# A transformer layer on one core: seven block products instead of eight for 7 of the 22 k-pairs of the down projection

## What is computed

```python
def conv_ffn(h, w_up, conv_w, conv_b, w_down):
    u = h @ w_up                                   # 2048 -> 11264
    ...
    a, b = jnp.split(u, 2, axis=-1)
    return (jax.nn.silu(a) * b) @ w_down           # 5632 -> 2048

def reference(x, ...):
    h = rms_norm(x, attn_norm[l]); p = h @ w_in[l]
    ...
    x = x + mix @ w_out[l]
    h = rms_norm(x, ffn_norm[l])
    x = x + conv_ffn(h, w_ffn_up[l], ffn_conv_w[l], ffn_conv_b[l], w_ffn_down[l])
```

## Time and profile before

| | |
|---|---|
| median of 3 runs | 1104.97 us (1104.68 to 1104.99) |
| span of the profiled execution, first to last instruction | 1103.2 us |
| PE busy | 1097.5 us, 99% of the span |
| DVE busy / ACT busy | 784.8 us (71%) / 586.6 us (53%) |
| down projection, first to last matmul start | 860.01 to 1099.14 us |
| from memory | 201.5 MB, 185 GB/s over the span |

### The profile page before, as it was taken

The page is one execution under the profiler, slowest core; times in us unless marked ns, Lnnn a source line. Parts: engine busy times, 40 slices in busy tenths (PEclk is TensorE's granted clock), DMA queues, the critical chain, the costliest instruction groups (busy, mean ns, idle before and its releaser), DMA issues.

```text
span 1103.2 us, 18805 instructions
## 1 busy us (share of the span) xinstructions
PE 1097.5 (99%) x6633; PEld 946.9 (86%) x6633; DVE 784.8 (71%) x1174; ACT 586.6 (53%) x863; POOL 26.8 (2%) x40
## 2 busy tenths in 40 slices
PE   9999999999999999999999999999999999999998
PEld 8888888888888888888888888888888888888887
DVE  6878988979656587878787878787878644454443
ACT  6677675766555555555455555555555433333332
POOL 4500000000000000000000000000000000000000
PEclk9999999999999999999999999999999999999999
DMA  7544556555555665556555565655555556656562
GB/s 260 188 153 145 162 173 190 166 183 172 181 183 167 191 196 189 188 190 190 190 190 190 184 191 183 191 185 190 188 190 190 191 191 198 208 195 214 193 210 76
DMA packets 172514, 204.26 MB, mean 185 GB/s; under 512 B 6949, under 2 KB 140470, under 8 KB 172214
## 3 DMA queue, kind: packets, MB, share of 16 engines
q1 hardware_dynamic: 171302, 201.55, 57.1%
q10 hardware_dynamic: 1168, 2.11, 0.6%
HBM read 201.54 MB, written 2.10 MB: 185 GB/s over the span
## 4 chain that ended last, share of the span: by engine, by line
PE 99%; DVE 1%; ACT 0%; issue 0%; DVEq 0%; ACTq 0%
PE bank L1344 37%; PE bank L1352 19%; PE bank L1398 10%; PE bank L1397 10%; PE bank L1396 10%; PE bank L1566 3%; PE bank L1567 3%; PE bank L1568 3%; PE bank L1310 1%; PE bank L1315 1%; PE bank L1605 0%; PE bank L1485 0%; PE bank L1373 0%; PE bank L1375 0%; PE bank L1376 0%; DVE hs L855 0%
## 5 line engine op out<-in xcount | busy, mean ns | idle before, releaser
L824 DVE TENSOR_TENSOR w_lo<-raw,w_hi 128x1024 fp32r<-128x1024 f32 x379 | 461.7, 1222 | 255.1 <-ACT w_hi L467 254.5
L467 ACT CAST w_hi<-raw 128x1024 fp32r<-128x1024 f32 x379 | 397.1, 1051 | 404.5 <-PE bank L1398 174.5
L1344 PE MATMUL bank<-hs,w_hi 128*128 128x512 f32 x1792 | 430.9, 391 | 0.0
L1344 PEld LDWEIGHTS bank<-hs,w_hi 128*128 128x128 f32 x1792 | 328.6, 188 | 64.1 <-issue 0.9
L1352 PEld LDWEIGHTS bank<-hs,w_lo 128*128 128x128 f32 x1792 | 230.1, 191 | 8.9 <-issue 0.2
L1352 PE MATMUL bank<-hs,w_lo 128*128 128x256 f32 x1792 | 233.9, 283 | 0.0
L1396 PE MATMUL bank<-w_hi,gated 128*128 128x512 f32 x352 | 136.9, 389 | 0.0
L1397 PE MATMUL bank<-w_lo,gated 128*128 128x512 f32 x352 | 136.9, 389 | 0.0
L1398 PE MATMUL bank<-w_hi,gated 128*128 128x512 f32 x352 | 136.9, 389 | 0.0
L1396 PEld LDWEIGHTS bank<-w_hi,gated 128*128 128x128 f32 x352 | 66.1, 188 | 13.8
L1397 PEld LDWEIGHTS bank<-w_lo,gated 128*128 128x128 f32 x352 | 66.1, 188 | 13.8
(11 more groups left out here) (188 smaller groups left out, 720.2 us busy)
## 6 DMA issues: line engine op xcount, KB each, us to landing
raw<-in_w_ffn_up_dram SPq DMA_DIRECT2D x176, 512.0 KB, 3.4
raw<-in_w_ffn_down_dram SPq DMA_DIRECT2D x88, 512.0 KB, 3.6
raw<-in_w_in_dram SPq DMA_DIRECT2D x52, 512.0 KB, 3.6
raw<-in_w_in_dram SPq DMA_DIRECT2D x64, 256.0 KB, 2.9
raw<-in_w_out_dram SPq DMA_DIRECT2D x32, 512.0 KB, 4.5
xt<-in_x_dram SPq DMA_DIRECT2D x2, 1024.0 KB, 6.6
out_dram<-xt ACTq DMA_DIRECT2D x3, 512.0 KB, 6.3
out_dram<-xt ACTq DMA_DIRECT2D x2, 256.0 KB, 2.5
```

The costliest lines, as they stand in the source:

```text
L467: act.copy(w_hi[:, i, :], raw[:, i, :]).then_inc(units_hi, 1)
L824: dve.tensor_tensor(w_lo[:, i, :], raw[:, i, :], w_hi[:, i, :].bitcast(F32), ALU.subtract)\
L1344: m = pe.matmul(banks[b][:, :], w_hi[:, i, c], hs[:, 4 * i + k, :], start=(first and k == 0), stop=(final and k == 3))
```

## The change

The output is now made as two pairs of column groups (`pair`, 1024 columns each). In a pair, four banks take two column blocks x two token halves, and k goes by in 22 k-pairs (`kp`, 2 k-tiles each; the code's `QUADRUPLES`). A unit is now 1 k-tile x 1024 columns, still 512 KB, and a k-pair is two units, a `four` or a `seven`:

- `four` (15 of 22): the two units are cast and split as before, and PE does 2 x 2 x 2 block products of three matmuls: 24 matmuls.
- `seven` (kp 6, 8, 10, 12, 14, 16, 18, in each of the two pairs): of the four weight blocks three are cast and split as they are (one operation of 128x1536 on ACT, one on DVE). DVE makes four sums of weight blocks (`t13` of 128x1024, then `t24` in two steps of 128x512), ACT casts them (`t_hi`), DVE makes their `lo` in place. PE does seven block products: 21 matmuls. Three of them are gathered over the pair in banks of their own (`bank_q5`, `bank_p6`, `bank_p7`, with `bank_p1` as the fourth) and merged into `xt` once a pair by DVE (`merge`, eight adds of 128x512).

The sums of activations that the sevens need (`s_hi`, `s_lo`) are made once, where `hs` stood, in four rounds (`sums_of_activations`, `hi_of_sums`, `lo_of_sums`): three in place of the k-pairs 1 to 3, which are split already, and the last after k-pair 4. The loops of the down projection are written out instead of being run by registers.

```diff
-            with sp.Fori(0, OUT_GROUPS // 2) as m:
...
+            for pair in range(COLUMN_PAIRS):
+                for kp in range(QUADRUPLES):
+                    for r in range(2):
+                        unit = first_unit_of(pair, kp) + r
+                        load_unit(unit // RING, unit % RING, w_down_v, 2 * kp + r, 1, pair * 2 * GT, 2 * GT)
...
+            def hi_of_sums(c):
+                act.wait_ge(s_made, c + 1)
+                n = min(2, SEVENS - 2 * c)
+                act.copy(s_hi[:, 2 * c:2 * c + n, :, :], sums[:, 0:n, :, :]).then_inc(s_rounded, 1)
+            def hi_of_plain(pair, kp):
...
+                act.wait_ge(loaded[i], loads_until(unit // RING) * 16)
+                act.wait_ge(loaded[i + 1], loads_until(unit // RING) * 16)
+                act.wait_ge(units_used, unit + 2)
+                act.copy(w_hi[:, i:i + 2, :].rearrange("p k n -> p (k n)")[:, GT:4 * GT],
+                         raw[:, i:i + 2, :].rearrange("p k n -> p (k n)")[:, GT:4 * GT]).then_inc(units_hi, 2)
+            def hi_of_summed(pair, kp):
...
+                act.wait_ge(t13_made, s + 1)
+                act.copy(t_hi[:, 0:2, :], t13[:, :, :]).then_inc(t13_hi, 1)
+                act.wait_ge(t4_made, s + 1)
+                act.copy(t_hi[:, 2:4, :], t24[:, :, :]).then_inc(t24_hi, 1)
...
+            for pair in range(COLUMN_PAIRS):
+                for kp in range(QUADRUPLES):
+                    if pair == 0 and kp < 4:
+                        if kp:
+                            hi_of_sums(kp - 1)
+                        continue
+                    hi_of(pair, kp)
+                    if pair == 0 and kp == 4:
+                        hi_of_sums(3)
+                    if kp == QUADRUPLES - 2:
+                        copy_partial(pair)
...
+            def lo_of_seven(pair, kp):
...
+                dve.wait_ge(units_hi, unit + 2)
+                dve.tensor_tensor(w_lo[:, i:i + 2, :].rearrange("p k n -> p (k n)")[:, plain],
+                                  raw[:, i:i + 2, :].rearrange("p k n -> p (k n)")[:, plain],
+                                  w_hi[:, i:i + 2, :].rearrange("p k n -> p (k n)")[:, plain].bitcast(F32),
+                                  ALU.subtract).then_inc(plain_split, 1)
...
+                dve.wait_ge(t_used, s)
+                dve.tensor_tensor(t13[:, :, :], quadruple[:, 1:3, :],
+                                  quadruple[:, 0:1, :].broadcast_to([P, 2, GT]), ALU.add).then_inc(t13_made, 1)
+                dve.wait_ge(t13_made, s + 1)
+                dve.sem_inc(units_split, 1)
+                dve.tensor_tensor(t24[:, 0, :], t13[:, 0, :], quadruple[:, 2, :], ALU.add).then_inc(t2_made, 1)
+                dve.wait_ge(t2_made, s + 1)
+                dve.tensor_tensor(t24[:, 1, :], t24[:, 0, :], quadruple[:, 3, :], ALU.add).then_inc(t4_made, 1)
+                dve.wait_ge(t13_hi, s + 1)
+                dve.tensor_tensor(t13_lo[:, :, :], t13[:, :, :], t_hi[:, 0:2, :].bitcast(F32), ALU.subtract)\
+                    .then_inc(t13_split, 1)
+                dve.wait_ge(t4_made, s + 1)
+                dve.sem_inc(units_split, 1)
+                dve.wait_ge(t24_hi, s + 1)
+                dve.tensor_tensor(t24_lo[:, :, :], t24[:, :, :], t_hi[:, 2:4, :].bitcast(F32), ALU.subtract)\
+                    .then_inc(t24_split, 1)
...
+            for pair in range(COLUMN_PAIRS):
+                for kp in range(QUADRUPLES):
+                    if pair == 0 and kp < 4:
+                        if kp:
+                            sums_of_activations(kp - 1)
+                            lo_of_sums(kp - 1)
+                        continue
+                    lo_of(pair, kp)
+                    if pair == 0 and kp == 4:
+                        sums_of_activations(3)
+                        lo_of_sums(3)
+                    if kp == QUADRUPLES - 2:
+                        merge(pair)
+                    if pair == 1 and kp == 0:
+                        add_last(0)
+            add_last(1)
...
+            def seven(pair, kp):
...
+                pe.wait_ge(plain_split, s + 1)
+                three(bank_p1(pair), *of_gated(2 * kp, 0), w_hi[:, i, c1], w_lo[:, i, c1], first, final)\
+                    .then_inc(units_used, 1)
+                three(bank_c(pair, 0, 1), *of_gated(2 * kp + 1, 0), w_hi[:, i + 1, c1], w_lo[:, i + 1, c1], False, False)
+                pe.wait_ge(s_split, n // 2 + 1)
+                three(bank_c(pair, 0, 0), *minus_sum_4, w_hi[:, i + 1, c0], w_lo[:, i + 1, c0], False, False)\
+                    .then_inc(units_used, 1)
+                pe.wait_ge(t13_split, s + 1)
+                three(bank_q5(pair), *sum_1, t_hi[:, 0, :], t13_lo[:, 0, :], first, final)
+                three(bank_p7(pair), *sum_3, t_hi[:, 1, :], t13_lo[:, 1, :], first, final)
+                pe.wait_ge(t24_split, s + 1)
+                three(bank_p6(pair), *sum_2, t_hi[:, 2, :], t24_lo[:, 0, :], first, final)
+                three(bank_c(pair, 1, 1), *of_gated(2 * kp + 1, 1), t_hi[:, 3, :], t24_lo[:, 1, :], False, False)\
+                    .then_inc(t_used, 1)
```

More of the change, by code:

```diff
@@ L798, in _ @@
             b_work(UP_GROUPS - 1, Q_DOWN + 1)
[L800 to L812, removed]
@@ L1710, in _, with three @@
                         unit_channels(g * 2 + ab + Q_UP, i, pair_of(G_UP + ab))
[L1713 to L1717, removed]
-                    if v == DOWN_UNITS - 1:
-                        pe.wait_ge(gated_lo, UP_GROUPS)
-                    unit_tokens(m * (2 * DOWN_UNITS // RING) + Q_DOWN + v // RING, v % RING,
-                                G_DOWN + n, gated, 2 * u, KT_FF, signal_first_tile=(u == DOWN_UNITS - 1))
+            def three(dst, x_hi, x_lo, hi, lo, start, stop):
+                pe.matmul(dst[:, :], x_hi, hi, start=start, stop=False)
+                pe.matmul(dst[:, :], x_hi, lo, start=False, stop=False)
+                return pe.matmul(dst[:, :], x_lo, hi, start=False, stop=stop)
@@ new lines, in of_gated, with four @@
+            def of_gated(tile, t):
+                return (gated[:, tile, t * P:(t + 1) * P], gated[:, tile, SEQ + t * P:SEQ + (t + 1) * P])
+            def four(pair, kp):
+                for r in range(2):
+                    unit = first_unit_of(pair, kp) + r
+                    i = unit % RING
+                    pe.wait_ge(units_split, unit + 1 + RING)
+                    for b in range(2):
+                        c = slice(b * GT, (b + 1) * GT)
+                        for t in range(TT):
+                            last = three(bank_c(pair, t, b), *of_gated(2 * kp + r, t), w_hi[:, i, c], w_lo[:, i, c],
+                                         kp == 0 and r == 0, kp == QUADRUPLES - 1 and r == 1)
+                            if kp == QUADRUPLES - 1 and r == 1 and (b, t) != LAST_BANKS[-1]:
+                                last.then_inc(bank_done, 1)
+                    last.then_inc(units_used, 1)
@@ new lines, in _ @@
+            for pair in range(COLUMN_PAIRS):
+                for kp in range(QUADRUPLES):
+                    if pair == 0 and kp == SEVEN_PRODUCTS[0]:
+                        pe.wait_ge(groups_evacuated, G_DOWN + BANK_PAIRS)
+                    if pair == 0 and kp == QUADRUPLES - 1:
+                        pe.wait_ge(gated_lo, UP_GROUPS)
+                    if pair == 1 and kp == 0:
+                        pe.wait_ge(merged, 1)
+                    if pair == 1 and kp == SEVEN_PRODUCTS[0]:
+                        pe.wait_ge(out_added, 4)
+                    if is_seven(kp):
+                        seven(pair, kp)
+                    else:
+                        four(pair, kp)
```

172 lines of the change are left out of this document (145 added, 27 removed).

## The result

| | before | after |
|---|---|---|
| median of the runs | 1104.9 us (5 runs, 1104.7 to 1105.0) | 1109.2 us (5 runs, 1108.8 to 1110.0) |
| span of the profiled execution | 1103.2 us | 1106.9 us |
| first and last matmul start of the down projection | 860.01, 1099.14 | 859.96, 1103.33 |

The ratio is 1.0041, with a 95% interval of 1.0030 to 1.0052: slower by 4.3 us, though PE has 42 matmuls less to do. The forecast was 1110.2 us, in a range of 1104.4 to 1117.

A forecast was written before the change was run, and what follows sets the result against it. The prediction took PE, busy 99% of the span, to bound the kernel. From 1104.97 us, -9.5 (matmuls), +8.1 (stop), +1.9 (clock), +0.2 (tail) and +4.5 (sevens) gave 1110.2 us, range 1104.4 to 1117.

The forecast's parts named there:

- What bounds the kernel, and the price of a matmul: PE, busy 99% of the span, bounds; 42 matmuls less in the down projection at 0.2267 us each: -9.5 us.
- The stop: PE stands still once ahead of unit 8, as three rounds of sums take 15.3 us against DVE's 8.4 lead: +8.1 us.
- the fourth round: Last round of sums, one k-pair, about 3 us, behind the split of units 8 and 9: 0 to 0.4 us.
- The clock: PE resumes at half clock after standing still at unit 8, for 3.8 us: +1.9 us, bounds 0 and 3.8.
- The sevens: Late second load makes the `raw` slot loop 10.65 us against PE's 10.20; ten waits of 0.45: +4.5 us, bounds 0 and 11.
- L: Landing time of a seven's second load, taken as 4.6 us; up to 4.2 PE would not wait.
- A page against the rows: Skill's 3.2 us for a 512 KB load gives a 9.2 us loop without PE waits; rows of paired loads contradict it.
- the rival of 1105.7: Pairs of loads land in time, up to 4.2 us, so the sevens run at PE's pace: 1105.7 us, chance 0.27.
- Hidden parts: `merge`, adding the first pair's four banks and ACT's 1 MB store stay covered among fours; written-out loops cost 0.
- The tail: Four stores of 256 KB at the end, issued 0.68 us apart, the last may queue: +0.2 us, bounds 0 and 0.8.
- The sum: Median before plus all terms: 1104.97 - 9.5 + 8.1 + 1.9 + 0.2 + 4.5 = 1110.2 us.

The follow-up runs named there:

- the layout run: Changed kernel with all 22 k-pairs as fours and no sums, merge or products of sums: 1103.9 us, ratio 0.9994 to the kernel before.
- both edits together: Changed kernel with rounds of sums among k-pairs 4 to 7 (13 sevens), and sums ahead of the plain `w_lo` in each seven: 1095.4 us, ratio 0.9919.
- the run with PE kept at work: Changed kernel plus 32 matmuls, result overwritten, that fill PE's stop ahead of unit 8: 1106.2 us, ratio 1.0013 to the kernel before.
- halves: Changed kernel with each down projection unit loaded by two transfers of 256 KB instead of one of 512 KB: 1105.7 us, ratio 1.0012.
- order: Changed kernel where DVE makes `t13` and `t24` ahead of the plain `w_lo` in a seven, both slots given back after it: 1105.4 us, ratio 1.0010.
- the rounds between units: Changed kernel with the four rounds of sums put between the units of k-pairs 4 to 7, 13 sevens: 1097.5 us, ratio 0.9931.

## Why the prediction was right, point by point

- **What bounds the kernel, and the price of a matmul.** Right. 0.2267 us for each of 42, found again in the layout run and in both edits together, where 39 matmuls less shorten the stage from 239.13 to 230.44 us. The recorded 0.39 would have promised 16.
- **The stop.** Right, mechanism and size: forecast 8.1, trace 8.23, and gone when the rounds are put elsewhere. The chain of 5.1 a round was exact because it was built from operations of the same sizes with their hand-overs. The last term, the fourth round, was put at 0 to 0.4, and 0 if PE is slow there. It cost nothing in the changed kernel; with PE kept at full clock, two starts at unit 10 were late by 0.26 us in all.
- **The clock.** Mechanism right (the run with PE kept at work), size too low: 1.9 against 2.44. I let the return take as long as the fall; PE worked 5.0 us at half clock. Three profiled executions of kernels with the same stop show 2.44, 1.82 and 1.59, all within the bounds of 0 and 3.8. What sets which of them comes stays open. So the time of the return was a guess, and that the term came within 0.5 us is partly luck.
- **The sevens.** The mechanism was right: held by the second load (halves), and by the cast that stands ahead of the sums in the loop (order). The size was off, 4.5 against 3.05, and that by errors that partly cancel. L was 4.34 instead of 4.6: the loads start 1.57 us apart, not 1.45, near the 4.3 of the pair at 1.6, and I had gone to the middle of the pairs. The rest of the loop was 6.2 instead of 6.0, with 0.15 us from the landing to the cast, a hand-over that I had left out. And each wait has a price behind it, 1.32 us in all, that no step had. Each seven that the load held waited 0.22 us on the mean where I had 0.45; part of a late `t13` is absorbed, since the weight load is ahead of its matmul (in the rows above it waited 0.42 us where the matmuls lost 0.16). The count of ten that the trace shows is partly luck. The loads held eight: in the first pair five, as many as forecast (though the second to the sixth and not the third to the seventh), in the second pair three: there one load took 3.5 us, one 4.0, and the lead still covered one of 4.4. The other two are the first of each pair, which I had rightly left out of the loop; what they wait for is the chain that begins when PE has used the slots of `w_hi`.
- **A page against the rows.** The Trainium skill (DMA: Bandwidth & Descriptors, section Anatomy of one DMA) gives 3.2 us for a 512 KB load, as an estimate, and by it there is no wait. A load alone took 3.4 here, near it. A load 1.57 us behind another took 4.34, and 5.4 at 0.4 us. There the measurement decides, and the rival of 1105.7 falls.
- **Hidden parts.** `merge`, `add_last`, the one store of 1 MB and the fourth round caused no wait of PE, and layout and loops cost nothing, as forecast. The store took 9.4 us to land and loads beside it up to 7.4, none of which reached PE. The tail was put at +0.2 and gave 0.5 back: the four stores start 0.61 to 0.68 us apart, they don't queue, and the last lands after 2.0 us where the same 256 KB took 2.5 before.
- **The sum.** 1110.2 forecast; the terms as the trace has them give 1104.97 - 9.5 + 8.2 + 2.4 + 3.1 - 0.5 = 1108.7, and the profiled execution took 1108.8. The median lies 0.4 above that. The main error, 1.5 us, is in the sevens; the clock and the tail are off by 0.5 and 0.7 in opposite directions.

## What to carry to other kernels

When a change takes work from the engine that bounds, add up what it lays on the engines that feed it at two scales: the total (DVE at 78%, harmless here) and the longest run of extra work that stands ahead of the next unit, against the lead in the ring (15.3 against 8.4 us, fatal here). Then follow one slot of the ring all the way round, load time included, and take out of that loop what needn't be in it; work that starts from the raw values should not stand behind a cast that it doesn't need. And measure the new loop against the period too: here it is still 0.1 to 0.2 us a seven too long, and only the lead hides it. 39 fewer matmuls were worth 9 us once both were put right; 42 fewer cost 4 where neither was.

## What the runs showed of the hardware that I had not expected

- **A load shortly behind another.** 512 KB alone: 3.4 to 3.5 us. Second of two on the same queue: 4.34 at a distance of 1.57 us (median of 14, from 3.5 to 4.6), 4.8 at 1.13 (median of 18, some with other transfers beside them), 5.4 to 5.5 at 0.4. Counted from the issue of the first that is 5.9, 5.9 and 5.8 us: the second arrives at about the same time however closely it follows. In four halves of 256 KB over the same distance of 1.57, the last took 3.5 (median) and was there 5.4 us after the first issue.
- **The matmuls behind a wait of PE.** The second start comes 0.08 to 0.11 us late, in ten sevens 1.03 us; the other 0.3 is hundredths at single later starts. Without the wait there is nothing of it. Its cause is open.
- **The clock's stretches differ.** After the same stop the half clock lasted 10.2 us in the changed kernel and 6.8 in the one with the other order, and in the latter it also fell later. The two stretches at half clock there, before and after PE resumed, the clock third from the right:

```profile
886.22:889.39 3.17, 0.00 (x1) 0.00 (x1) 2.42 (x3) 2.61 (x3) 0.00 (x0) 0.50 0.01 3
889.39:893.05 3.66, 3.66 (x9) 2.89 (x10) 2.87 (x6) 0.83 (x2) 0.00 (x0) 0.50 0.64 163
```

PE worked there for 3.7 us at half clock instead of 5.0. The mean clock of single runs shows the same two lengths: 0.995 or 0.997 over the span in each of the 25 runs with the long stop. In the halves the times fall apart by it: five runs at 0.997 took 1104.8 to 1105.2 us, five at 0.995 took 1106.1 to 1106.4. So some 1.3 us are decided anew in every run of it; in the other two kernels with the stop the two groups overlap. It isn't the only spread: without any stop, the rounds between units took 1095.5 to 1097.8, with sevens that still wait, while the kernels in which PE hardly waits spread over 0.2 to 0.6.
